# A dense expert mixer whose weighted sum over v is made of three rounded fp32 passes instead of one true fp32 product

## The reference

```
idx = ...                              # 8 x 16 of 16384 experts a token, by product keys
g   = softmax(best_s)
ue, ve = u[idx], v[idx]
act = gelu(einsum('cd,chkd->chk', x, ue))
out = einsum('chk,chkd->cd', g * act, ve)
```

## Time and profile before

| | us |
|---|---|
| median of 3 runs | 5217.56 |
| lowest, highest | 5213.93, 5222.57 |
| the profiled execution | 5214.52 |
| its span, first to last instruction | 5212.7 |
| TensorE busy, of the span | 4361.0 (84%) |
| VectorE busy | 3454.1 (66%) |
| GpSimd busy | 1825.8 (35%) |
| ScalarE busy | 1212.6 (23%) |
| mean granted clock of TensorE | 0.919 |

### The profile page before, as it was taken

One profiled execution on the slowest core, in us unless ns is written; L12 is line 12 of the kernel. 1 busy time (PEld: TensorE's weight loads), 2 busy tenths in 40 slices (PEclk: granted clock), 3 DMA queues, 4 the chain that ended last, 5 costly groups with the idle time before them and its releaser, 6 DMA issues. The chain is left out here.

```text
span 5212.7 us, 54609 instructions
## 1 busy us (share of the span) xinstructions
PE 4361.0 (84%) x18847; PEld 2971.3 (57%) x18847; DVE 3454.1 (66%) x7226; ACT 1212.6 (23%) x2191; POOL 1825.8 (35%) x1652
## 2 busy tenths in 40 slices
PE   5799985793887799999999957886737777999997
PEld 4476764483555466666666625553433435666665
DVE  2256665468988877776777745675588775666665
ACT  0223321110343311111111112331212332222222
POOL 0021112022666655554555500000126774343441
PEclk9899978897999899999999979997868889999999
DMA  7577764612899999999999946667318999999995
GB/s 251 188 226 210 224 191 137 223 62 94 328 374 346 332 374 359 356 358 343 369 356 359 350 129 187 193 167 203 125 65 313 339 336 359 356 355 357 356 358 196
DMA packets 514294, 1407.95 MB, mean 270 GB/s; under 512 B 45661, under 2 KB 128605, under 8 KB 509183
## 3 DMA queue, kind: packets, MB, share of 16 engines
q1 hardware_dynamic: 329726, 733.60, 43.3%
q0 software_dynamic: 184320, 671.17, 34.0%
HBM read 1226.33 MB, written 178.26 MB: 269 GB/s over the span
## 5 line engine op out<-in xcount | busy, mean ns | idle before, releaser
L1623 POOL DMA_INDIRECT expert_rows<-u_rows,peer_arena x640 | 893.1, 1395 | 1311.3 <-DVE expert_rows L1897 1049.2
L1668 PE MATMUL ps<-part_arena,peer_part_arena 128*128 128x384 f32 (+1 forms) x4096 | 1034.7, 335 | 29.5 <-DVE peer_part_arena L1940 27.6
L1897 DVE SCALAR_TENSOR_TENSOR expert_rows<-expert_rows,mixer_in 128x1024 f32<-128x1024 f32 x640 | 759.9, 1220 | 125.0 <-DMA expert_rows<-u_rows,peer_arena 121.8
L1640 PE MATMUL ps<-expert_rows,peer_arena 128*128 128x512 f32 x1024 | 540.3, 680 | 329.8 <-DVE peer_arena L1905 327.5
L1630 POOL DMA_INDIRECT expert_rows<-in_peer_v,peer_arena x640 | 729.4, 1140 | 195.1 <-issue 186.0
L1668 PEld LDWEIGHTS ps<-part_arena,peer_part_arena 128*128 128x128 f32 x4096 | 698.4, 189 | 92.4 <-issue 77.6
L1677 PE MATMUL ps<-best,peer_arena 128*128 128x512 f32 x1540 | 685.3, 592 | 0.0
L1668 PE MATMUL ps<-mixer_in_parts,peer_part_arena 128*128 128x384 f32 (+1 forms) x2048 | 632.9, 309 | 0.0
L1640 PEld LDWEIGHTS ps<-expert_rows,peer_arena 128*128 128x128 f32 x1024 | 212.4, 217 | 602.4 <-issue 311.7
L1924 DVE SCALAR_TENSOR_TENSOR peer_arena<-expert_rows,peer_arena 128x1024 f32<-128x1024 f32 x381 | 489.4, 1285 | 30.5 <-DVE peer_arena L1924 2.3
L1450 POOL TENSOR_TENSOR part_arena<-peer_arena,part_arena 128x1024 fp32r<-128x1024 f32 x32 | 76.4, 2390 | 1077.8 <-ACT part_arena L1427 1077.8
(11 more groups left out here) (250 smaller groups left out, 6212.9 us busy)
## 6 DMA issues: line engine op xcount, KB each, us to landing
peer_arena<-in_peer_u SPq DMA_DIRECT2D x256, 512.0 KB
best<-in_peer_v SPq DMA_DIRECT2D x154, 512.0 KB
mixer_arena<-in_peer_u SPq DMA_DIRECT2D x296, 256.0 KB, 7.5
u_rows<-mixer_arena SPq DMA_DIRECT2D x148, 512.0 KB, 6.3
hidden<-in_peer_u SPq DMA_DIRECT2D x216, 256.0 KB, 6.3
u_rows<-hidden SPq DMA_DIRECT2D x108, 512.0 KB, 4.8
gates<-peer_arena SPq DMA_DIRECT2D x20, 2048.0 KB
peer_arena<-in_peer_v SPq DMA_DIRECT2D x52, 512.0 KB
```

The lines of the kernel that those rows point to most:

```text
L1623: pool.indirect_dma_start(u_ring[:, k % U_SLOTS, :], None, u_table, bass.IndirectOffsetOnAxis(u_index[s][:, m:m + 1], 0)).then_inc(u_row_i ...
L1640: mm = pe.matmul(ps[:, 2 + half, :], diag[m % V_SLOTS], v_ring[:, m % V_SLOTS, half * 512:half * 512 + 512], start=m == 0, stop=m == PAIRS ...
L1668: mm = pe.matmul(ps[:, 6, 0:dense_tok], left[j % len(left)][:, c, :], right[:, c, :], start=at == 0, stop=at == len(todo) - 1)
L1897: dve.scalar_tensor_tensor(out=rows, in0=rows, scalar=1.0, in1=B.x[:, :, rows_at + s * P:rows_at + s * P + P], op0=ALU.mult, op1=ALU.mult, ...
```

## The change

- `values(j)` makes three products of rounded parts, `Y_PASSES`: w_high v_high, w_high v_low, w_low v_high. In place of 4 or 6 true fp32 matmuls (8 or 12 instructions) there are 12 or 18 fp32r ones, 512 columns each.
- ScalarE makes `v_high` (`round_v`, 1024 columns, into two buffers, after values(j-2) is done) and `w_high` (`round_w`, 384 or 256 columns, as soon as wt(j) is there). The order in a step is now gelu(j), round_w(j), round_u(j+2), round_v(j+1).
- VectorE makes `w_low` between wt(j) and split_u(j+2), and waits for `round_w(j)` in front of it.
- GpSimd makes `v_low` (`split_v`, 1024 columns), at fixed places among the gathers that `splits_at` and `LEAD` give: one every two gathers of u and of v in layer 0, one after each in layer 1.
- values(j) waits for v_low(j) and w_low(j).
- u and v have four buffers instead of five.

```diff
-    BUFS = 5
+    BUFS, LEAD = 4, ns + 3
...
-    v_space = [ar.take(D)] + [B.best[:, x * D:x * D + D] for x in range(3)] + [B.spare_arena[:, 3 * D:]]
-    v = v_space[:BUFS]
+    v = [B.best[:, x * D:x * D + D] for x in range(3)] + [B.spare_arena[:, 3 * D:]]
+    v_low = [B.best_r[:, x * D:x * D + D] for x in range(3)] + [B.part_arena[:, 3 * D:]]
...
+    Y_PASSES = ((w_high, v_high), (w_high, v_low), (w_low, v_high))
...
+    def splits_at(k):
+
+        return sum(PAIRS + (ns - 1) * PAIRS * max(0, j - 1) // KEYS + LEAD <= k for j in range(KEYS))
...
     def gpsimd(pool):
+        def split_v(j):
+            pool.wait_ge(v_rounded, j + 1)
+            pool.tensor_tensor(v_low[j % BUFS], v[j % BUFS], v_high[j % 2].bitcast(F32), ALU.subtract).then_inc(v_split, 1)
+
+        split = 0
         for k in range(steps):
             s, m = divmod(k, PAIRS)
+            while split < splits_at(k):
+                split_v(split)
+                split += 1
...
+        for j in range(split, KEYS):
+            split_v(j)
...
         def values(j):
-            pe.wait_ge(v_in[j % BUFS], 16 * (j // BUFS) + 16)
-            pe.wait_ge(wt_ok, j + 1)
+            pe.wait_ge(v_split, j + 1)
+            pe.wait_ge(w_split, j + 1)
             for n in range(nd):
                 for half in range(2):
-                    mm = pe.matmul(ps[:, 2 * n + half, :], wt[j % 2][:, n * P:n * P + P], v[j % BUFS][:, half * 512:half * 512 + 512],
-                                   start=j == 0, stop=j == KEYS - 1)
+                    for at, (left, right) in enumerate(Y_PASSES):
+                        mm = pe.matmul(ps[:, 2 * n + half, :], left[j % 2][:, n * P:n * P + P],
+                                       right[j % len(right)][:, half * 512:half * 512 + 512],
+                                       start=j == 0 and at == 0, stop=j == KEYS - 1 and at == 2)
...
+        def round_v(j):
+            act.wait_ge(v_in[j % BUFS], 16 * (j // BUFS) + 16)
+            if j >= 2:
+                act.wait_ge(y_mm, j - 1)
+            act.copy(v_high[j % 2], v[j % BUFS]).then_inc(v_rounded, 1)
+
+        def round_w(j):
+            act.wait_ge(wt_ok, j + 1)
+            act.copy(w_high[j % 2], wt[j % 2]).then_inc(w_rounded, 1)
...
         for j in range(2):
             round_u(j)
+            round_v(j)
...
             act.activation(gelu[j % 2], ps[:, 6, 0:dense_tok], ACT.Gelu).then_inc(act_ok, 1)
+            round_w(j)
             if j + 2 < KEYS:
                 round_u(j + 2)
+            if 1 <= j < KEYS - 1:
+                round_v(j + 1)
...
             if j >= 2:
                 dve.wait_ge(y_mm, j - 1)
+                dve.wait_ge(w_split, j - 1)
             dve.tensor_tensor(wt[j % 2].rearrange("p (n t) -> p n t", t=TG), gelu[j % 2].rearrange("p (n t) -> p n t", t=TG),
                               g[j // QUAD % 2][:, :, j % QUAD, :], ALU.mult).then_inc(wt_ok, 1)
+            dve.wait_ge(w_rounded, j + 1)
+            dve.tensor_tensor(w_low[j % 2], wt[j % 2], w_high[j % 2].bitcast(F32), ALU.subtract).then_inc(w_split, 1)
             if j + 2 < KEYS:
                 split_u(j + 2)
```

More of the change, by code:

```diff
@@ L195, in build @@
         B.part_arena = sb("part_arena", PART_ARENA, F32R)
+        with nc.sbuf_tensor("best_parts", [P, BEST], F32R) as whole:
+            B.best_r = whole
         B.best = sb("best", BEST)
@@ L1527, in peer @@
     u = [ar.take(C * P).rearrange("p (c i) -> p c i", c=C) for _ in range(BUFS)]
-    v_space = [ar.take(D)] + [B.best[:, x * D:x * D + D] for x in range(3)] + [B.spare_arena[:, 3 * D:]]
-    v = v_space[:BUFS]
+    v = [B.best[:, x * D:x * D + D] for x in range(3)] + [B.spare_arena[:, 3 * D:]]
+    v_low = [B.best_r[:, x * D:x * D + D] for x in range(3)] + [B.part_arena[:, 3 * D:]]
     g = [ar.take(QUAD * dense_tok).rearrange("p (n j t) -> p n j t", j=QUAD, t=TG) for _ in range(2)]
-    gelu, wt = ([ar.take(dense_tok) for _ in range(2)] for _ in range(2))
+    gelu = [ar.take(dense_tok) for _ in range(2)]
+    wt_at = ar.at
+    wt = [ar.take(dense_tok) for _ in range(2)]
     parts = Arena(B.peer_arena_r)
@@ L1534, in peer @@
     u_high = [parts.take(C * P).rearrange("p (c i) -> p c i", c=C) for _ in range(2)]
+    v_high = [parts.take(D) for _ in range(2)]
+    parts.at = 0
+    w_high = [parts.take(dense_tok) for _ in range(2)]
+    parts.at = wt_at
+    w_low = [parts.take(dense_tok) for _ in range(2)]
     parts.at = at
@@ L1545, in peer @@
              "g_out0", "g_out1", "g_in0", "g_in1",
-             "s_mm", "act_ok", "wt_ok", "y_mm", "x_split", "u_rounded", "u_split", "back_mm", "added", "y_ev")
+             "s_mm", "act_ok", "wt_ok", "y_mm", "x_split", "u_rounded", "u_split", "v_rounded", "v_split", "w_rounded", "w_split", "back_mm", "added", "y_ev")
     (iota_in, shifted, exp_ok, chosen_ok, chain_s, passed, score_ok, gelu_ok, diag_ok, s0_mm, s0_ev,
@@ L1549, in peer @@
      g_out0, g_out1, g_in0, g_in1,
-     s_mm, act_ok, wt_ok, y_mm, x_split, u_rounded, u_split, back_mm, added, y_ev) = (B.sem(x) for x in names)
+     s_mm, act_ok, wt_ok, y_mm, x_split, u_rounded, u_split, v_rounded, v_split, w_rounded, w_split, back_mm, added, y_ev) = (B.sem(x) for x in names)
     g_out, g_in = (g_out0, g_out1), (g_in0, g_in1)
```

## The result

| | before | after |
|---|---|---|
| median us | 5215.75 (4 runs) | 5545.93 (4 runs, 5539.03 to 5548.45) |
| ratio | | 1.063, 95% interval 1.061 to 1.0647 |
| span of the profiled execution | 5212.7 | 5546.7 |
| mean granted clock of TensorE | 0.919 | 0.904 |
| layer 0: mean distance from wt to wt, 127 of them | 9.35 | 10.51 |

Slower by 6.3%, 330 us. The forecast was 5472 with a range of 5270 to 5600. The two dense loops hold all of it: 127 x (10.51 - 9.35) = 147 us and 127 x (7.76 - 6.26) = 190 us, 337, against 334 us between the spans.

A forecast was written before the change was run, and what follows sets the result against it. TensorE was taken to bound the dense loops before; after, VectorE's step held by GpSimd's subtraction: 5214.5 + 147 (layer 0) + 106 (layer 1) + 5 (start) gave 5472 us, range 5270 to 5600.

The forecast's parts named there:

- TensorE's value matmuls: Dense loops: rounded matmuls at 0.235 us each, TensorE's steps 8.45 and 5.65 us, 196 us less over both layers.
- VectorE's own step in layer 0: Layer 0 dense loop: VectorE's step with w_low and two new waits, before any hold by GpSimd, 8.32 us.
- The exclusion, 2.2 us: Dense loops: each GpSimd subtraction of v keeps VectorE out of SBUF, adding 2.2 us except what falls into VectorE's waits.
- rival A: Dense loops: faster, VectorE hardly held; 5112 us with the DMA as bound, 5018 without; chance 0.15.
- Layer 0, 10.5 us: Layer 0 dense loop: subtraction enters ahead of the spread, nothing covered; 8.32 + 2.20 = 10.5 us a step, +147 us.
- Layer 1, 7.1 us: Layer 1 dense loop: two subtractions per two steps, partly covered by VectorE's waits; 7.1 us a step, +106 us.
- The start and first steps: Start of both layers: v roundings ahead of tile 0's copy, first subtraction behind the first gathers; +5 us together.
- B: Dense loops: slower but little, GpSimd always enters at the new waits, which cover it; 5273 us, chance 0.18.
- C: Dense loops: worse, every entry costs the full 2.40 us with nothing covered; 5600 us, chance 0.10.
- The signs: Dense stretches: VectorE instruction 2.2 us longer, TensorE busy about 80%, chain over VectorE and GpSimd, steps 10.5 and 7.1 us.
- A sum: Layer 0 dense loop: GpSimd's gathers of 5.7 us with the subtraction make 8.4 of 9.37 us, so it has room.

The follow-up runs named there:

- e1: Changed kernel without GpSimd's subtraction of v (second values pass reads v_high, v_low's share left out): 5029.85 us, ratio 0.9657 to the kernel before.
- e9: Changed kernel with GpSimd's subtraction cut into four of 256 columns: 5486.85 us.
- e7: Changed kernel whose GpSimd subtraction also waits for this step's wt, to enter where VectorE waits for w_high: 5405.31 us.
- e2: Changed kernel with v_low made by VectorE instead of GpSimd, ahead of the wait for w_high: 5036.82 us, ratio 0.9654 to the kernel before.
- e5: Changed kernel with GpSimd filling v_low with zero in place of the subtraction, nothing read: 5026.22 us.
- e3: Changed kernel with GpSimd's subtraction over 512 of the 1024 columns, half of v_low's share left out: 5268.81 us.
- e8: Changed kernel with GpSimd copying v_high into v_low's place instead of subtracting, one operand read: 5240.06 us.
- e6: Kernel before, with four buffers and one unused GpSimd subtraction of 128x1024 per step: 5207.65 us, beside 5205.61 of the kernel before.
- e4: Changed kernel with values by true fp32 matmuls of w_high and v_high alone, all splits still made: 5542.62 us.

## Why the prediction was right, and where it was off

- **TensorE's value matmuls** were taken at 0.235 us from the score rows and took 0.231. The steps of e1, 8.43 and 5.73 us, stand beside the 8.45 and 5.65 of the text. The estimate by the Trainium skill's formula for lone matmuls ("TensorE: Matmul & The Clock Gate", Back-to-back issue gap), 216 ns here, is 7% under what was measured.
- **VectorE's own step in layer 0** was worked out from start to start as 8.32 us. In e1, with both waits in it, it is 2307.63 - 2299.32 = 8.31.
- **The exclusion, 2.2 us.** Held by 2.20 us in layer 0, by 2.1 to 2.2 in layer 1. That the spread and the products are scalar_tensor_tensor and that no row of before showed them held was rival A's case; they are held like the others (L1937 3.42 for 1.22).
- **Layer 0, 10.5 us:** 10.51, and 147 us as forecast. But the step on where GpSimd gets in failed. The prediction had it enter only where VectorE drains, so ahead of the spread. It entered behind split_u, in front of the first product, between two instructions of VectorE that otherwise follow one another without a gap. In the first kind of e9's steps it gets in between them several times. The sum did not depend on it, because neither place has a wait to hide it.
- **Layer 1, 7.1 us:** 7.70. This is the term that was mis-sized, and nearly all of the 73 us that the forecast lacks. The prediction took some 0.5 us of cover at each entry, at the waits of w_low and split_u, and more behind the second: (11.08 + 4.40 - 0.98)/2 and less. With no cover, (11.08 + 4.40)/2 = 7.74. GpSimd stood ready during the spread and needed no drain: it entered ahead of wt, one instruction too early for the waits. The mistaken belief on the entry, harmless in layer 0, is what cost the accuracy here. e7 shows that waits can be hidden: with the entry put at w_low's wait, layer 1 ran at 7.23 us and both layers saved 141 us. In layer 1 it was the wait behind w_low that went, though, and not the one ahead of it.
- **The start and first steps,** +5 us in the text: 337 us in the loops against 334 between the spans leave nothing that can be told from zero.
- **The rivals.** A needed VectorE not to be held, and it was. Its bound by the DMA was also wrong, for it took the 369 GB/s of the earlier trace rows as the most the DMA can do, 9.0 and 5.9 us a step; e2 moved 396 GB/s with steps of 8.46 and 5.80. The time that A gave without that bound, 5018, is near what the kernel reaches once GpSimd no longer reads v (5026 in e5, 5030 in e1, 5037 in e2). B, entry always at the waits, is what e7 makes by force, yet at 5405 and not 5273: B took 1.1 us of cover for each entry, e7 got 0.86 in layer 0, 0.60 in the mean, and (7.76 - 7.23) x 2 = 1.06 for a pair of steps with two entries in layer 1. C had the covers right (none) and the length too high: 2.2 us, not 2.4. Its 5600 us, given a chance of 0.10, is nearer to the measured 5546 than the forecast's 5472: 54 us against 74. It was the width of the range, drawn to hold C's end, that left room for the missing covers.
- **The signs.** The longer instruction, the 10.5 us and the 0.231 us came as named. The chain does not lead over GpSimd (0% of it), and TensorE was busy for 85% and 81% where 80% was named.
- **A sum.** GpSimd's own step with the subtraction is 5.7 + 2.4 = 8.1 us by the earlier trace rows, and not the 8.4 of the text. Nothing rests on it, since either is under 9.37.

What stays open: which gathers are late in e7 and e9, and behind what, and why four quarters that start in a wait don't hand the turn over while those that start beside a working VectorE do. Neither was tried.

## What to carry to other kernels

Work moved to GpSimd is not beside VectorE's if it reads SBUF while VectorE works on two SBUF tensors: add nearly its whole length to VectorE's step (0.3 us less here, in e3, e8 and the changed kernel), then subtract VectorE's slack (e6: 2.7 us of slack in layer 0 made it free) and the waits that it hides: what it covers of the wait in which it enters, and a wait that ends while the held instruction stands (0.43 and 0.39 us in e7). Here the subtraction cost 516 us on GpSimd, which looked idle. On VectorE, where it took half as long and fitted into waits, it cost 7 us, less than the spread of the runs. Before a split is given to the emptier engine, look at what the busy one waits for.

## What was not expected of the hardware

- GpSimd needs no pause of VectorE to get its turn: it got in between two back-to-back VectorE instructions (3.42 us at 2504.52). The row of the GLA mixer in which it stood outside a chain is not the rule.
- Four short instructions of GpSimd in a row took turns with VectorE's when they began beside a working VectorE (1.09 and 1.13 us for 0.55 and 0.56, 66 times), and ran back to back over one VectorE instruction when they began in VectorE's wait (3.03 us for 0.56, 40 times).
- What GpSimd does with SBUF decides: a fill of 128x1024 (0.96 us) held nothing, a copy of one operand (1.15 us) held a product for 0.84 us.
- The DMA moved 396 GB/s over 900 us at a share of 1.03, 27 above the busiest stretch seen before.
- TensorE's mean granted clock fell from 1.00 to 0.96 and 0.93 in the two stretches, where it had begun to idle; score matmuls behind 1.93 us of idle time ran at the lower level (0.50, 1.2 GHz), 0.31 us apart. In layer 0 nothing hung on it: e4 had 1.00 in layer 0's stretch and took the same time.
